# First expert's gate as a plain fp32 product, second expert's gate weights split ahead, up weights asked for before down weights

## The reference, cut to what matters

```
tok = rmsnorm(h, norm_ffn)                      # 1032 rows of 1024
def expert_block(xb, e):
    hid = silu(xb @ w_gate[e]) * (xb @ w_up[e])    # w_gate, w_up: 1024 x 512
    return hid @ w_down[e]                         # w_down: 512 x 1024
out = segment_sum(gate_s * ybuf[dest], tok_s)   # every token: its two experts
```

## Time and profile before

| | us |
|---|---|
| median of 3 executions | 1159.6 |
| lowest, highest | 1157.82, 1159.95 |
| the profiled execution | 1158.35 |
| its span | 1156.5 |
| PE busy | 1124.8 (97%) |
| DVE busy | 827.9 (72%) |
| ACT busy | 643.6 (56%) |
| mean DMA rate | 253 GB/s |

### The profile page before, as it was taken

One profiled execution on the slowest core, in us unless ns is written; L12 is line 12 of the kernel. 1 busy time (PEld: TensorE's weight loads), 2 busy tenths in 40 slices (PEclk: granted clock), 3 DMA queues, 4 the chain that ended last, 5 costly groups with the idle time before them and its releaser, 6 DMA issues.

```text
span 1156.5 us, 17522 instructions
## 1 busy us (share of the span) xinstructions
PE 1124.8 (97%) x7034; PEld 884.0 (76%) x7034; DVE 827.9 (72%) x1181; ACT 643.6 (56%) x796; POOL 110.7 (10%) x131
## 2 busy tenths in 40 slices
PE   7999999999999999999899999999999999999995
PEld 6999999999957768887577777777777777777762
DVE  5414435223377658888988898898898888988886
ACT  7221241211068733334687777777777777778844
POOL 1002110012000000000031000111100111012110
PEclk9999999999999999999999999999999999999999
DMA  7216474433050051115899999999999999999867
GB/s 240 73 38 189 130 247 138 144 98 122 2 180 24 26 222 74 74 73 209 329 403 405 381 394 387 386 398 379 384 390 380 381 393 385 387 385 373 330 263 299
DMA packets 77941, 292.49 MB, mean 253 GB/s; under 512 B 9702, under 2 KB 34406, under 8 KB 52962
## 3 DMA queue, kind: packets, MB, share of 16 engines
q1 hardware_dynamic: 65010, 255.55, 58.4%
q0 software_dynamic: 11680, 31.57, 8.3%
q10 hardware_dynamic: 1168, 4.23, 0.9%
HBM read 270.09 MB, written 33.77 MB: 263 GB/s over the span
## 4 chain that ended last, share of the span: by engine, by line
PE 92%; DVE 4%; ACT 1%; DMA 1%; issue 1%; SPq 0%; ACTq 0%; DVEq 0%; POOLq 0%
PE psum L1224 10%; PE psum L1223 10%; PE psum L1222 10%; PE psum L859 8%; PE psum L861 8%; PE psum L860 8%; PE psum L1251 5%; PE psum L1253 5%; PE psum L1252 5%; PE psum L994 3%; PE psum L996 2%; PE psum L995 2%; PE psum L1211 2%; PE psum L944 2%; PE psum L960 1%; PE psum L938 1%
## 5 line engine op out<-in xcount | busy, mean ns | idle before, releaser
L859 PE MATMUL psum<-h_hi,w_hi 128*128 128x344 f32 (+2 forms) x576 | 185.8, 323 | 3.0 <-DVE h_lo L1738 2.9
L861 PE MATMUL psum<-h_hi,w_lo 128*128 128x344 f32 (+2 forms) x576 | 184.0, 319 | 0.0
L860 PE MATMUL psum<-h_lo,w_hi 128*128 128x344 f32 (+2 forms) x576 | 183.9, 319 | 0.0
L2194 DVE TENSOR_TENSOR w_down_lo<-w_down,w_down_hi 128x2048 fp32r<-128x2048 f32 x62 | 139.7, 2289 | 41.9 <-ACT w_down_hi L1549 41.6
L2194 DVE TENSOR_TENSOR w_gate_lo<-w_gate,w_gate_hi 128x2048 fp32r<-128x2048 f32 x64 | 144.3, 2289 | 17.7 <-ACT w_gate_hi L1549 17.6
L2194 DVE TENSOR_TENSOR w_up_lo<-w_up,w_up_hi 128x2048 fp32r<-128x2048 f32 x64 | 143.7, 2286 | 2.1
L1549 ACT CAST w_gate_hi<-w_gate 128x2048 fp32r<-128x2048 f32 x64 | 120.0, 1920 | 9.4 <-DMA w_gate<-in_w_gate 9.2
L1549 ACT CAST w_up_hi<-w_up 128x2048 fp32r<-128x2048 f32 x64 | 120.4, 1926 | 3.4 <-DMA w_up<-in_w_up 3.2
L1549 ACT CAST w_down_hi<-w_down 128x2048 fp32r<-128x2048 f32 x62 | 115.8, 1911 | 2.4 <-DMA w_down<-in_w_down 2.4
L859 PEld LDWEIGHTS psum<-h_hi,w_hi 128*128 128x128 f32 x576 | 108.2, 188 | 5.5 <-DVE h_lo L1738 3.8
L861 PEld LDWEIGHTS psum<-h_hi,w_lo 128*128 128x128 f32 x576 | 108.2, 188 | 0.0
(11 more groups left out here) (310 smaller groups left out, 1925.1 us busy)
## 6 DMA issues: line engine op xcount, KB each, us to landing
w_gate<-in_w_gate SPq DMA_DIRECT2D x64, 1024.0 KB, 17.3
w_up<-in_w_up SPq DMA_DIRECT2D x64, 1024.0 KB, 17.2
w_down<-in_w_down SPq DMA_DIRECT2D x64, 1024.0 KB, 15.4
w_raw<-in_w_in SPq DMA_DIRECT2D x24, 512.0 KB, 4.4
y_tile<-y_rows SPq DMA_DIRECT2D x16, 512.0 KB, 10.9
kv<-in_cache_k POOLq DMA_DIRECT2D x24, 256.0 KB, 4.5
kv<-in_cache_v POOLq DMA_DIRECT2D x24, 256.0 KB, 4.5
x_tile<-in_x_prompt SPq DMA_DIRECT2D x8, 512.0 KB, 5.2
```

What stands on the lines that cost most here:

```text
L859: mm(ps, wh[:, k, :], h_hi[:, k, cols], start=(k == 0), stop=False)
L860: mm(ps, wh[:, k, :], h_lo[:, k, cols], start=False, stop=False)
L861: ins = mm(ps, wl[:, k, :], h_hi[:, k, cols], start=False, stop=(k == KD - 1))
L2194: vec.tensor_tensor(dst[:, part, :], src[:, part, :], hi[:, part, :].bitcast(F32), ALU.subtract).then_inc(split, 1)
```

## The change

The first expert's gate product no longer uses split operands. ACT copies the turned first rows from PSUM to `xT_first` (fp32, in the space of `wd[1]`), and TensorE multiplies them with the raw weights `wg[0]` in plain fp32, one matmul per block (`first_plain`). The split of these weights falls away on ACT and DVE; `wg_hi` is free from the start, so ACT and DVE split the gate weights of the second expert there ahead of the loop, and the loop's first turn has no gate split. The first up product becomes an ordinary `up`. `lower_rows(first, 0)` moves behind the split of the first up weights. SP asks for up weights 1 before down weights 0, and for down weights 1 only when the first gate product is done. The semaphore `all_sent` is replaced by a further step of `pool_step`; it is waited for only in a branch for experts with more than 96 rows.

```diff
+        xT_first = at("xT_first", unit(6) + 4096, [KD, SLOTS])
...
             sp.wait_ge(pool_step, 3)
+            load_up(first, 1, 1)
             load_down(first, 0, 0)
-            load_up(first, 1, 1)
             store_residual(NT - 1)
-            sp.wait_ge(first.xT_ready, 2)
+            sp.wait_ge(first.gate_done, 1)
             load_down(first, 1, 1)
...
-            def gate_or_up(hi, lo, b, split, xT_lo_done, n, done):
+            def gate_or_up(hi, lo, b, split, xT_lo_done, n, done, plain):
 
                 for k in range(KD):
                     if k % 4 == 0:
-                        pe.wait_ge(split, 2 * n + (k // 4 + 1))
+                        pe.wait_ge(split, 2 * (n - plain) + (k // 4 + 1))
...
-            first_upper(wg_hi, 0, first.gate_hi)
-            first_upper(wu_hi, 1, first.up_hi)
+            def first_plain(w, b, landed, done):
+
+                for k in range(KD):
+                    if k % 4 == 0:
+                        pe.wait_ge(landed[k // 4], 16)
+                        pe.wait_ge(plain_rows, k // 4 + 1)
+                    ins = mm(bank(b)[0:SLOTS, :], xT_first[:, k, :], w[:, k, :], start=(k == 0), stop=(k == KD - 1))
+                ins.then_inc(done, 1)
+
+            first_plain(wg[0], 0, first.gate_in[0], first.gate_done)
             count_all()
-            first_lower(wg_lo[0], 0, first.gate_split, first.gate_done)
-            first_lower(wu_lo[0], 1, first.up_split, first.up_done)
+            up(first, 0, 0)
...
             act.wait_ge(o_ready, 4 * NT)
-            upper_gate(0)
             upper_up(0)
+            upper_weight(wg_hi, wg[1], KD, first.gate_hi, first.gate_in[1], 16, (0,))
+            for half in range(2):
+                act.wait_ge(first.xT_ready, half + 1)
+                nc.scalar.copy(xT_first[:, 4 * half:4 * half + 4, :],
+                               bank(4 + half)[:, 0:4 * SLOTS].rearrange("p (k t) -> p k t", k=4)
+                               ).then_inc(plain_rows, 1)
             act.wait_ge(h2_out[1], 16 * 4)
             upper_rows(first, 0)
+            upper_weight(wg_hi, wg[1], KD, first.gate_hi, first.gate_in[1], 16, (1,))
...
-            lower_rows(first, 0)
             step(experts_of(NT - 2))
...
-            lower_gate(first, 0, 0)
             lower_up(first, 0, 0)
+            lower_rows(first, 0)
+            lower_gate(first, 1, 1)
             count_all()
             finish_gates()
             for b in range(NE + 1):
...
                 if b + 1 < NE:
-                    lower_gate(first, (b + 1) % 2, b + 1)
+                    if b >= 1:
+                        lower_gate(first, (b + 1) % 2, b + 1)
                     lower_rows(first, b + 1)
```

More of the change, by code:

```diff
@@ L391, in program @@
         gates_ready = sem("gates_ready")
-        all_sent = sem("all_sent")
+        plain_rows = sem("plain_rows")
         chosen_ready = sem("chosen_ready")
@@ L776, in _ @@
                                      ).then_inc(first.down_in[0][h], 16)
-                sp.wait_ge(all_sent, 1)
+                sp.wait_ge(pool_step, 4)
                 for t in range(NT):
@@ L1227, in gate @@
             def gate(f, s, n):
-                gate_or_up(wg_hi, wg_lo[s], 0, f.gate_split, f.xT_lo_done, n, f.gate_done)
+                gate_or_up(wg_hi, wg_lo[s], 0, f.gate_split, f.xT_lo_done, n, f.gate_done, 1)
             def up(f, s, n):
-                gate_or_up(wu_hi, wu_lo[s], 1, f.up_split, f.xT_lo_done, n, f.up_done)
+                gate_or_up(wu_hi, wu_lo[s], 1, f.up_split, f.xT_lo_done, n, f.up_done, 0)
             def turn_hidden(f, n):
@@ L1254, in down @@
                 ins.then_inc(f.y_done, 1)
-            def first_upper(hi, b, hi_ready):
+            def first_plain(w, b, landed, done):
                 for k in range(KD):
                     if k % 4 == 0:
[L1260 to L1273, removed]
+                        pe.wait_ge(landed[k // 4], 16)
+                        pe.wait_ge(plain_rows, k // 4 + 1)
+                    ins = mm(bank(b)[0:SLOTS, :], xT_first[:, k, :], w[:, k, :], start=(k == 0), stop=(k == KD - 1))
                 ins.then_inc(done, 1)
-            first_upper(wg_hi, 0, first.gate_hi)
-            first_upper(wu_hi, 1, first.up_hi)
+            first_plain(wg[0], 0, first.gate_in[0], first.gate_done)
             count_all()
-            first_lower(wg_lo[0], 0, first.gate_split, first.gate_done)
-            first_lower(wu_lo[0], 1, first.up_split, first.up_done)
+            up(first, 0, 0)
             for b in range(NE + 1):
@@ L1541, in upper_rows, with upper_weight @@
                                    ).then_inc(f.xT_hi_done, 1)
-            def upper_weight(dst, src, chunks, ready, landed, count):
+            def upper_weight(dst, src, chunks, ready, landed, count, halves=(0, 1)):
                 half = chunks // 2
-                for c in range(2):
+                for c in halves:
                     part = slice(c * half, (c + 1) * half)
@@ L1566, in upper_gate @@
             def upper_gate(n):
-                if n >= 1:
+                if n >= 2:
                     act.wait_ge(first.gate_done, n)
@@ L1601, in _ @@
                 if b + 1 < NE:
-                    upper_gate(b + 1)
+                    if b >= 1:
+                        upper_gate(b + 1)
                     upper_rows(first, b + 1)
@@ L2197, in lower_gate @@
             def lower_gate(f, s, n):
-                lower_weight(wg_lo[s], wg[s], wg_hi, KD, f.gate_hi, n, f.gate_split)
+                lower_weight(wg_lo[s], wg[s], wg_hi, KD, f.gate_hi, n - 1, f.gate_split)
             def lower_up(f, s, n):
@@ L2397, in _ @@
                     pool.wait_ge(first.sent, 16 * o + 16 * NE)
-            gp.memset(stat[0:1, 95:96], 0.0).then_inc(all_sent, 1)
+            gp.memset(stat[0:1, 95:96], 0.0).then_inc(pool_step, 1)
 _OUT = {
```

## The result

The changed kernel takes 1161.34 us (median of 20 executions, 1158.55 to 1164.77), the kernel before 1158.93 in the same session (20 executions, 1157.62 to 1160.56). The ratio is 1.0020, 95% interval 1.0014 to 1.0026: **slower by 2.4 us**, outside the forecast range, where 1157.4 was forecast. The profiled execution of the changed kernel took 1161.48 us, span 1159.6.

A forecast was written before the change was run, and what follows sets the result against it. TensorE (97% busy) and DMA were taken as both full in the expert stage. The second gate gains 3.4 us, but gate three's weights limit the gain to 2.2: from 1159.6 to 1157.4, range 1154.6 to 1160.8.

The forecast's parts named there:

- TensorE, ACT and DVE: Expert two's gate on these engines: starts at 564.0, 3.4 us earlier, with another 1.6 back if the clock holds.
- The 16 halves: First expert's plain fp32 gate product on TensorE: 16 half matmuls of 512 columns take 6.9 us.
- The gate split of expert two: DVE's split of the second expert's gate weights, behind up split and rows: done at 561.0.
- The second gate: Second expert's gate product on TensorE: starts at 564.0, 3.4 us earlier, after an idle of 0.8.
- ACT's silu: First silu of expert one on ACT: ACT is ready at 556.7, the silu needs the gate at 557; all hidden.
- The room at the last experts: TensorE's start on the last expert: 2.7 us of room, so the gain of 2.2 passes, 5 would not.
- SP and the transfers: Third expert's gate weights: queue full, landing unmoved, so the third gate starts at 584.44, 2.2 us earlier than now.
- down two behind the first gate: SP's wait for the first gate holds back down two; 4.7 MB keep the queue full until about 564, no hole.
- the order of the two first requests: Up two and down one exchanged in SP's queue: the same transfers stand ahead of gate three, landing unmoved.
- the rival at 0.2: Clock falls in the 2.7 us idle before the third gate, which takes 1.6 more: gain 0.6, 1159.0; chance 0.2.
- The rival for a slower result: Gate four's earlier request shares the queue, gate three up to 5.2 us later: 1162.6, with clock 1164.2; chance 0.08.

The follow-up runs named there:

- the gap filled: Changed kernel with SP asking for the second expert's up weights before its wait for POOL: 1154.42 us, ratio 0.9961 to the kernel before.
- the rows first: Changed kernel with `lower_rows(first, 0)` moved back ahead of the up split: 1159.92 us, ratio 1.0004 to the kernel before.

## Why the prediction was wrong

**TensorE, ACT and DVE: right.** The 16 halves took 7.03 us recorded, up followed, and the rows of expert two were turned at +12.62 (forecast 12.6). The gate split of expert two was done at 561.6, 561.0 with the shift taken off. The second gate started after 0.92 (forecast 0.8) at +14.37 (forecast 14.04), with the clock kept, and took 5.6. ACT's silu waited for nothing but the plain product. The room at the last experts was not touched: from the third gate's end on the two kernels take the same 564.3 us. With the gap filled and the rows first a lead of 4.6 us reached the end whole (third gate ends at +37.7, then 564.3), but there the queue runs ahead as well, so the forecast bound of 2.7 was not put to the test.

**SP and the transfers: here it failed**, in the words "the queue has been full since 552.64, when the first down weights are released by POOL's fetch, and that release does not move". It moved by 1.84 us. The prediction counted POOL's instructions, found them the same, and took for granted that its fetch lasts as long as before whatever DVE does beside it. Its own numbers held the cause: it moves `xT_lo` behind the up split and starts that split at 551.3, and the fetch of before starts at 551.53 and ends at 552.52, so fetch and split would start in the other order. The trace of before could have said what that costs. There POOL's next transfers, at 563.79, 582.07 and 588.78, took 1.63, 2.73 and (a transfer of results) 6.36 us. All three started within a half of a split; most others take 0.94 to 0.97. With the release 1.84 later the second half's cast ended at 584.23, 583.61 without the shift, and not at the 581.65 of before; the wait became 4.33. The other request that the change holds back, down two behind the first gate, did what was forecast: with the rows first, where it waits in the same way, the DMA share is 0.94 or more in every stretch from 554 to 590, so no hole opens.

That the order of the two first requests changes nothing was right for gate three's landing and wrong for TensorE: it gathers the waits in one.

**The clock: the rival at 0.2 was the likelier case.** The prediction put a wait of 2.7 nearer to 1.8, which had kept the clock, than to 4.4, which had not. With the wait at 2.62, as forecast, the clock fell, and at 2.02 as well, each in the one execution that was profiled. Waits of 1.56 and less kept it. The price was 1.6 for these, as the rival said, and 2.6 behind the wait of 4.33.

**The sum.** Forecast +34.5 for the third gate in 5.6 us; measured +36.6 in 8.2. Late requests cost 1.7 of it (rows first brings the start from 36.6 to 34.9), the clock 2.6 (1.0 of it because the late requests made the wait longer: 8.2 us against 7.2), and some 0.4 is left with the rows first too, where ACT starts on the weights' second half 0.3 later than in before; why is not shown. In medians, moving the rows back is worth 0.16%, moving the requests back 0.09% (within the intervals), both 0.33%, which leaves a gain of 0.13% in place of the loss of 0.20%. The rival for a slower result (gate four's request sharing the queue) had the sign right and the mechanism wrong: with the gap filled, gate four is asked for just as early, and the third gate comes early all the same.

## What to carry to other kernels

A queue that waits for another engine's instruction inherits all that can lengthen it: before moving a long DVE instruction, look which POOL instruction then runs beside it, and who waits for that one. A lead on one engine is worth only what the next resource lets through; look for a stretch in which that one lies empty and put its next request there. And count TensorE's idle time by the piece: here 3.7 us in three pieces cost no clock, and 2.0 in one did, in one profile each.

## What the hardware showed that was not expected

A DVE difference with both operands in SBUF that is under way when POOL's indirect fetch starts holds it up until a DVE instruction ends, and the fetch then takes about its full length: 2.76 us in place of 0.99. It is no matter of this one place. Of the 63 indirect transfers of POOL in the kernel before, 16 start within a half of a split; 15 of them end 0.8 to 0.9 us after the end of that half, whatever they had waited. The 47 others take 0.91 to 0.99 us, but for the last, 1.15. The sixteenth started in the second half of the up split, let the two halves of the down split behind it pass as well, and took 6.36:

```profile
588.78 6.36 POOL L2329 DMA_INDIRECT y_rows<-y_rows,sidx  x1 [3.98 <-ACT y_rows L1564]
```

Why some transfers slip in between two halves (the one at 563.79) and this one did not is not shown.

The Trainium skill (SBUF — State Buffer, Who interferes with whom) says that a VectorE instruction with two SBUF inputs contends with a GpSimd instruction that reads SBUF, and that the one to start second is blocked. The traces agree where the fetch is the second, if the fetch, which takes its row numbers from SBUF, counts as such an instruction. The other way round they show no block: the split that starts 0.3 us before the end of the fetch in the kernel before takes its usual 4.49. The same section reports that `tensor_tensor` had not stalled a DMA; here it did, for 1.8 us.
